# Two narrow full-precision products of a decoder step spread over four column groups of TensorE

## The reference

```python
# layer 0: 16 "rank" columns, widened to 512 by a second matrix
q, k, v, r, a_lr = jnp.split(x @ w_in, [QK_W, 2 * QK_W, 2 * QK_W + V_W, 2 * QK_W + 2 * V_W], axis=-1)
log_a = jax.nn.log_sigmoid((a_lr @ w_a2 + b_a).astype(F32)) / GLA_TAU
...
# layer 1: 16 gate columns, 8 for the input gate and 8 for the forget gate
q, k, v, o_pre, g_pre = jnp.split(x @ w_in, [QK_W, 2 * QK_W, 2 * QK_W + V_W, 2 * QK_W + 2 * V_W], axis=-1)
g = GATE_CAP * jnp.tanh((g_pre + b_gate).astype(F32) / GATE_CAP)
i_pre = g[..., :MLSTM_HEADS]
log_f = jax.nn.log_sigmoid(g[..., MLSTM_HEADS:])
```

## Time and profile before

| | |
|---|---|
| median of three runs | 1518.46 us |
| profiled execution | 1519.5 us, of which 1517.7 us are the span of its instructions |
| PE busy | 1500.7 us, 99% |
| DVE busy | 1216.1 us, 80% |
| ACT busy | 1010.2 us, 67% |
| DMA | 449.97 MB, 296 GB/s on average |
| granted TensorE clock | 0.997 of full on average |

### The profile page before, as it was taken

The page is one execution under the profiler, slowest core; times in us unless marked ns, Lnnn a source line. Parts: engine busy times, 40 slices in busy tenths (PEclk is TensorE's granted clock), DMA queues, the critical chain, the costliest instruction groups (busy, mean ns, idle before and its releaser), DMA issues.

```text
span 1517.7 us, 22956 instructions
## 1 busy us (share of the span) xinstructions
PE 1500.7 (99%) x8499; PEld 1189.8 (78%) x8499; DVE 1216.1 (80%) x1182; ACT 1010.2 (67%) x872; POOL 189.8 (13%) x229
## 2 busy tenths in 40 slices
PE   9999999999999999999999999999999999999997
PEld 7999999999998977777777776776776776777775
DVE  6858766646767588888888888888888888888888
ACT  5646533325556487787787777777778778778776
POOL 3334200002235140000000000000000000000010
PEclk9999999999999999999999999999999999999999
DMA  7467555455444689999999999999999999999993
GB/s 217 141 202 235 165 168 169 162 171 183 140 136 132 244 305 379 378 354 392 376 343 394 376 358 382 376 367 376 379 374 362 379 380 360 377 381 354 390 372 130
DMA packets 234263, 449.97 MB, mean 296 GB/s; under 512 B 16712, under 2 KB 83344, under 8 KB 234208
## 3 DMA queue, kind: packets, MB, share of 16 engines
q1 hardware_dynamic: 226208, 422.98, 77.9%
q0 software_dynamic: 7376, 24.53, 5.6%
q10 hardware_dynamic: 624, 1.70, 0.3%
HBM read 434.62 MB, written 14.57 MB: 296 GB/s over the span
## 4 chain that ended last, share of the span: by engine, by line
PE 93%; DVE 4%; ACT 1%; issue 1%; DMA 0%; SPq 0%; DVEq 0%; ACTq 0%
PE bank L1105 29%; PE bank L1107 28%; PE bank L1106 28%; PE bank L1762 1%; PE bank L1353 1%; DVE ring_lo L2314 1%; PE bank L1342 0%; PE bank L1696 0%; PE bank L1676 0%; PE bank L1791 0%; DMA par_rows<-in_mlstm_g_norm_dram 0%; DVE work L2273 0%; PE bank L1333 0%; PE bank L1254 0%; PE bank L1661 0%
## 5 line engine op out<-in xcount | busy, mean ns | idle before, releaser
L2906 DVE TENSOR_TENSOR w_lo<-ring,w_hi 128x2048 fp32r<-128x2048 f32 x337 | 771.4, 2291 | 121.4 <-ACT w_hi L2181 119.9
L2181 ACT ACTIVATE w_hi<-ring 128x2048 fp32r<-128x2048 f32 x337 | 645.4, 1918 | 223.3 <-PE bank L1107 223.2
L1105 PE MATMUL bank<-w_hi,xg_hi 128*96 128x512 f32 x896 | 355.6, 397 | 1.0 <-DVE xg_lo L2916 1.0
L1107 PE MATMUL bank<-w_hi,xg_lo 128*96 128x512 f32 x896 | 353.8, 395 | 0.0
L1106 PE MATMUL bank<-w_lo,xg_hi 128*96 128x512 f32 x896 | 351.6, 392 | 0.0
L1107 PE MATMUL bank<-work_split,ring_lo 128*128 128x288 f32 x920 | 270.7, 294 | 0.0
L1105 PE MATMUL bank<-work_split 128*128 128x288 f32 x904 | 268.6, 297 | 0.9 <-DVE ring_lo L2358 0.4
L1106 PE MATMUL bank<-work_split 128*128 128x288 f32 x904 | 265.9, 294 | 0.0
L1107 PEld LDWEIGHTS bank<-w_hi,xg_lo 128*96 128x96 f32 x896 | 144.4, 161 | 62.9
L1105 PEld LDWEIGHTS bank<-w_hi,xg_hi 128*96 128x96 f32 x896 | 144.5, 161 | 61.3 <-DVE w_lo L2906 2.0
L1106 PEld LDWEIGHTS bank<-w_lo,xg_hi 128*96 128x96 f32 x896 | 145.0, 162 | 59.9
(11 more groups left out here) (463 smaller groups left out, 1670.9 us busy)
## 6 DMA issues: line engine op xcount, KB each, us to landing
ring<-in_moe_w_gu_dram SPq DMA_DIRECT2D x225, 1024.0 KB, 6.6
ring<-in_moe_w_down_dram SPq DMA_DIRECT2D x112, 1024.0 KB, 6.4
ring<-in_ffn_w_gu_dram SPq DMA_DIRECT2D x22, 1024.0 KB, 5.1
ring<-in_gla_w_in_dram SPq DMA_DIRECT2D x12, 1024.0 KB, 5.5
ring<-in_mlstm_w_in_dram SPq DMA_DIRECT2D x12, 1024.0 KB, 5.3
ring<-in_ffn_w_down_dram SPq DMA_DIRECT2D x8, 1024.0 KB, 5.1
out_dram<-work POOLq DMA_DIRECT2D x9, 512.0 KB, 4.6
work<-in_state_gla_S_dram POOLq DMA_DIRECT2D x8, 512.0 KB, 7.2
```

Source lines behind the costliest of these rows:

```text
L1105: pe.matmul(out, w_hi_, x_hi, start=first, stop=False, skip_group_check=True)
L1107: return pe.matmul(out, w_lo_, x_hi, start=False, stop=last, skip_group_check=True)
L2181: ac.activation(w_hi[:, j % SPLIT, :], src, ACT.Copy).then_inc(whi_ready, 1)
L2906: ve.tensor_tensor(w_lo[:, j % SPLIT, :], src, w_hi[:, j % SPLIT, :].bitcast(F32), ALU.subtract)\
```

## The change

Both narrow products become `group_rows`. Block kt is multiplied by a weight of 32 columns, and its result goes to column group kt mod 4, PSUM partitions 32 (kt mod 4) to 32 (kt mod 4) + 31. So each product leaves four partial sums. Columns 16 to 31 of the weight are zero.

In layer 0 the four partial sums are summed by the next product: ACT copies all 128 rows, `w_a2` is loaded eight times, one below the other, and L0z is 128 rows deep. In layer 1 ACT copies the 128 rows, and one product with a wider `fold` sums them and puts the forget gates at partition 32; it is placed inside key tile k0, behind its block 3 (12 of 24 matmuls). DVE then reads this product's bank.

The weights of the two products share one buffer. The gate weights come in one small load instead of four, behind load 10 and after a wait for the rank rows. Seven more copies of `w_a2` are small loads of SP ahead of load 3. POOL fills zero columns once more at the start and makes the wider `fold` with four more steps.

```diff
         else:
             pj("g")
+            use("L1gf", 4)
             pj("k0")
...
-        fold = sb("fold", [P, MH])
+        fold = sb("fold", [P, GATE_ROW + MH])
...
-        w_lr = sb("w_lr", [P, KT, RANK])
-        w_gate = sb("w_gate", [P, KT // 4, 2, 4, MH])
-        w_a2 = sb("w_a2", [RANK, QK])
+        w_lr = sb("w_lr", [P, KT, GROUP])
+        w_gate = w_lr
+        w_a2 = sb("w_a2", [P, QK])
...
-        lr_sb = rank_rows[0:RANK, 9, :]
-        den_sb = rank_rows[:, 9, :]
+        lr_sb = rank_rows[:, 9, :]
+        den_sb = lr_sb
...
-                    small(w_lr[:, :, :], ins["gla_w_in"][0, :, 3072:3088].rearrange("(t p) n -> p t n", p=P))
-                    small(w_a2[:, :], ins["gla_w_a2"][0])
+                    small(w_lr[:, :, 0:RANK], ins["gla_w_in"][0, :, 3072:3088].rearrange("(t p) n -> p t n", p=P))
+                    for r in range(P // RANK):
+                        small(w_a2[r * RANK:(r + 1) * RANK, :], ins["gla_w_a2"][0])
...
-                if 4 <= i < 8:
-                    a, g = divmod(i - 4, 2)
-                    small(w_gate[:, a, g, :, :], ins["mlstm_w_in"][0, a * 4 * P:(a + 1) * 4 * P, 3072 + g * MH:3072 + (g + 1) * MH]
-                          .rearrange("(t p) n -> p t n", p=P), late_loaded)
+                if i == 10:
+                    sp.wait_ge(*full("L0lr"))
+                    small(w_gate[:, :, 0:2 * MH], ins["mlstm_w_in"][0, :, 3072:3072 + 2 * MH].rearrange("(t p) n -> p t n", p=P), late_loaded)
...
+            c(gp.memset(w_lr[:, :, RANK:GROUP], 0.0))
...
+            def group_rows(bk, w, l):
+
+                for kt in range(KT):
+                    pe.wait_ge(h_ready, KT * l + kt + 1)
+                    r = kt % 4 * GROUP
+                    mm = pe.matmul(bk[r:r + GROUP, 0:T], w[:, kt, :], hT[:, kt, :], start=(kt < 4), stop=(kt >= 4), skip_group_check=True)
                 return mm
...
-            end(rows_of(bk, w_lr, hT, 0, KT, RANK), "L0lr")
+            end(group_rows(bk, w_lr, 0), "L0lr")
...
-            for kt in range(KT):
-                pe.wait_ge(h_ready, KT + kt + 1)
-                mm = pe.matmul(bk[0:GATE_ROW + MH, 0:T], w_gate[:, kt // 4, :, :, :].rearrange("p g c n -> p (g c n)")
-                               [:, kt % 4 * MH:kt % 4 * MH + GATE_ROW + MH], hT[:, kt, :], start=(kt == 0), stop=(kt == KT - 1))
-            normed[0] = None
-            end(mm, "L1g")
-            for m in range(4):
+            end(group_rows(bk, w_gate, 1), "L1g")
+
+            def fold_gates():
+
+                pe.wait_ge(*copied("L1g"))
+                pe.wait_ge(fold_ready, N_FOLD)
+                bk = begin("L1gf")
+                end(pe.matmul(bk[0:GATE_ROW + MH, 0:T], fold[:, :], lr_sb[:, :], start=True, stop=True), "L1gf")
+
+            qk_tile("L1", "k", 0, {3: fold_gates})
+            for m in range(1, 4):
                 qk_tile("L1", "k", m)
...
-            free(ac.activation(lr_sb[:, :], take("L0lr")[0:RANK, 0:T], ACT.Copy), "L0lr")
+            free(ac.activation(lr_sb[:, :], take("L0lr")[:, 0:T], ACT.Copy), "L0lr")
...
-            ac.wait_ge(*copied("L1g"))
+            free(ac.activation(lr_sb[:, :], take("L1g")[:, 0:T], ACT.Copy), "L1g")
+            ac.wait_ge(*copied("L1gf"))
...
-            bk = take("L1g")
+            bk = take("L1gf")
```

More of the change, by code:

```diff
@@ L555, in trunk_kernel @@
         out_stored = sem("out_stored")
-        N_CONST = 42
+        N_CONST = 43
         N_FIRST = 5
-        N_FOLD = 5
-        N_SMALL = 16 * 8
-        N_LATE = 16 * 12
+        N_FOLD = 9
+        N_SMALL = 16 * (7 + P // RANK)
+        N_LATE = 16 * 9
         S_DONE = 16 * S_FIRST
@@ L905, in make_fold @@
                 gp.memset(fold[:, :], 0.0).then_inc(fold_ready, 1)
-                for r in range(4):
-                    gp.wait_ge(fold_ready, r + 1)
-                    gp.affine_select(out=fold[:, :], in_=fold[:, :], compare_op=ALU.not_equal, fill=1.0, base=-GROUP * r,
-                                     pattern=[[-1, MH]], channel_multiplier=1).then_inc(fold_ready, 1)
+                n = 1
+                for g in range(2):
+                    out = fold[:, GATE_ROW * g:GATE_ROW * g + MH]
+                    for r in range(4):
+                        gp.wait_ge(fold_ready, n)
+                        gp.affine_select(out=out, in_=out, compare_op=ALU.not_equal, fill=1.0, base=-(GROUP * r + MH * g),
+                                         pattern=[[-1, MH]], channel_multiplier=1).then_inc(fold_ready, 1)
+                        n += 1
+                assert n == N_FOLD
             def add_squares(i):
@@ L1074, in _ @@
                 end(mm, f"x{kt}")
-            normed = [None]
             def norm_of_sum(i, name):
@@ L1082, in norm_of_sum @@
                 end(pe.matmul(bk[:, 0:T], ones[:, :], hT[:, 0, :], start=True, stop=True), name)
-                normed[0] = i // 2
             def norm(i, name):
@@ L1091, in norm @@
                 end(mm, name)
-                normed[0] = i // 2
-            def rows_of(bk, w, src, c, n, m):
-                for kt in range(n):
-                    if normed[0] is not None:
-                        pe.wait_ge(h_ready, KT * normed[0] + kt + 1)
-                    mm = pe.matmul(bk[0:m, 0:T], w[:, kt, c:c + m], src[:, kt, :], start=(kt == 0), stop=(kt == n - 1))
-                normed[0] = None
+            def group_rows(bk, w, l):
[3 more added lines that the diff above has]
+                    mm = pe.matmul(bk[r:r + GROUP, 0:T], w[:, kt, :], hT[:, kt, :], start=(kt < 4), stop=(kt >= 4), skip_group_check=True)
                 return mm
@@ L1139, in first_tile, with qk_tile @@
                 end(sq, "L0ss")
-                normed[0] = 0
             qk_weights = [None]
-            def qk_tile(l, which, m):
+            def qk_tile(l, which, m, inside={}):
                 g = 2 * int(l[1])
@@ L1155, in qk_tile @@
                                kt == 0, kt == KT - 1)
+                    if kt in inside:
+                        inside[kt]()
                 end(mm, f"{l}{which}{m}")
@@ L2603, in _ @@
             mixer_lo(2, 3)
-            bk = take("L1g")
+            bk = take("L1gf")
             ve.tensor_scalar(rows[:, 0, :], bk[0:MH, 0:T], b_i[:, 0:1], None, ALU.add)
-            free(ve.tensor_scalar(rows[:, 1, :], bk[GATE_ROW:GATE_ROW + MH, 0:T], b_f[GATE_ROW:GATE_ROW + MH, 0:1], None, ALU.add), "L1g")
+            free(ve.tensor_scalar(rows[:, 1, :], bk[GATE_ROW:GATE_ROW + MH, 0:T], b_f[GATE_ROW:GATE_ROW + MH, 0:1], None, ALU.add), "L1gf")
             ve.wait_ge(tanh_ready, 2)
```

## The result

The changed kernel takes 1522.88 us (median of 18 runs, 1520.02 to 1526.22). 18 runs of the kernel before, beside it, have a median of 1520.28 us (1518.34 to 1522.91). The ratio is 1.0019, 95% interval 1.0012 to 1.0026: slower by 2.6 us, against the forecast of 0.9 us faster. The time lies above the stated range of 1515.7 to 1519.7, and above the 1521.5 from which on the prediction had 5%. The profiled execution took 1524.22 us, its span is 1522.4 us, and its mean granted clock is 0.993 against 0.997.

A forecast was written before the change was run, and what follows sets the result against it. The prediction took DVE's releases to bound the kernel. The median 1518.46 us less 0.87 from layer 0, or the profiled 1519.5 less 2.09 with the clock, gave 1517.5 us, with layer 1 adding nothing; range 1515.7 to 1519.7.

The forecast's parts named there:

- What bounds the kernel: Whole kernel: DVE's releases set the pace although PE is busy 1500.7 of 1517.7 us, so saved PE time becomes waiting.
- The grouped product: Rank rows and gate rows: 16 records in four column groups take 1.01 us, saving PE 2.98 and 3.00 us.
- the rival without overlap: Both narrow products: column groups do not overlap, layer 0 gives nothing, and the result is 1518.7 us; 5% chance.
- drains at a switch of tiling mode: Both grouped products: each pays two drains, which lie in pauses PE has anyway, so the sum stays.
- Layer 0: Before k0: PE waits about 2 us for DVE's weight slot, k0 starts 0.87 us earlier, and L0z costs the same.
- No fall at k1: Layer 0, k1: the 128-row L0z may remove the clock's fall; 1.56 us for PE, both effects 2.09 us at most.
- So the 0.87 us should arrive at layer 1.: From layer 0 to layer 1: PE and DVE both move by 0.87 us and the lead lasts.
- Layer 1, the release: Before layer 1's k0: DVE's weight slot at 380.24 releases it, so k0 starts 1.22 us earlier after a 1.7 us pause.
- it costs nothing, with 1.8 us of cover: Layer 1, inside k0: folded rows are ready at about 382.7 us, before DVE asks at 384.50.
- the new pauses lower the clock: Rival: the pause before layer 0's k0 brings the lower clock, k0 takes 1.56 us longer, result 1519.2 us; 16% chance.
- the base: Starting time of the sum: the kernel before at 1518.46 us, the median of three runs, taken as without the clock's fall.
- SP: Load queue at the start: seven more small issues at 0.43 us each, 3.0 us in all, stay hidden.

The follow-up runs named there:

- same_layout_fill: The full change with the work area kept at its old address, plus five products of constants in layer 1's pause; 1517.77 us, ratio 0.9988 to the kernel before.
- fill_layer1: The full change plus five products of constants between layer 1's gate rows and k0; 1521.44 us, ratio 1.0008 to the kernel before.
- fold_wide: The kernel before with only the fold buffer widened to 40 columns, moving later buffers by 128 bytes; 1522.14 us, ratio 1.0014.
- same_layout: The full change with the wide fold matrix placed elsewhere, so the work area keeps its old address; 1520.37 us, ratio 0.9996 to the kernel before.
- two_blocks: The kernel before with layer 1's gate product over two of its eight blocks, without groups, copy or fold product; 1520.45 us, ratio 1.0002.
- layer0_only: The kernel before with only layer 0's part of the change, layer 1 and the fold matrix as before; 1518.91 us, ratio 0.9987.
- layer1_only: The full change with layer 0's rank rows summed in one group and w_a2 loaded once; 1524.50 us, ratio 1.0029 to the kernel before.
- deep_rank: The kernel before with only L0z made 128 rows deep and w_a2 loaded eight times; 1520.14 us, ratio 0.9996.
- layer0_192: The kernel before with layer 0's part of the change and the work area 192 bytes along; 1519.63 us, ratio 0.9995.

## Why the prediction was wrong

*What bounds the kernel.* Right. Nearly all that TensorE saves turns into waits for DVE, in both layers, and neither the full 6 us nor a part of 3 us reached the end in any kernel.

*The grouped product.* Right: 16 records within 1.18 us in both layers. From its first record to the start of a product that follows without a pause it takes 1.11 us (same_layout_fill, 378.76 to 379.87), against 1.01 forecast and 3.99 before. That excludes the rival without overlap. The rule of the Trainium skill, "TensorEngine Tiling (Array Packing)", section "Key Properties", on drains at a switch of tiling mode was put as harmless to the sum. The trace agrees that a switch costs time, and little: behind the grouped product the first full-width record of fill_layer1 starts 0.34 us after the last grouped one and its own successor 0.35 us later, where such records otherwise are 0.24 apart. That is 0.2 us for the way back. The kernel before paid as much between its rank rows and k0 (0.34 and 0.24 us, where 0.24 and 0.13 are usual), so the sum stays.

*Layer 0.* Right in mechanism, with one term missed. The pause was 1.78 us and ended by line 2321, the counterpart of 2314. k0 came 1.02 us nearer (forecast 0.87). L0z was put at the same cost within 0.1 us, and that is the term: the reading that depth isn't dearer holds for the single record, but going to the 16-row form and back cost 0.39 us. No fall at k1, as hoped. The lead came to 2.3 us against 2.09. (By the prediction's own working the clock alone would be worth 1.22 us to vt4, 63.59 less 62.37, and not 1.25.)

*"So the 0.87 us should arrive at layer 1."* **This step failed**, by way of a term that the sum didn't have. The lead shrank by 2.0 us between 136 and 379 us, because the widened fold matrix moved the split weights by 128 bytes and each of the some 75 tiles there grew by 0.027 us. fold_wide shows this alone at 1.0014, and same_layout shows the change without it at 0.9996, where the forecast had 0.9994. The prediction costed what each edit executes and nothing for where its buffers lie.

*Layer 1, the release.* **Wrong in its releaser.** The prediction had k0 wait for the weight slot at 380.24. It is held by DVE's second read-out of q2, whose bank k0 takes, and which in the kernel before ended at 381.19. It lies in the stretch that the earlier trace rows leave out, between 378.04 and 384.50:

```profile
380.73 0.46 DVE L2591 TENSOR_TENSOR work<-bank,rbc 64x288 f32<-64x288 f32 x1
```

So k0 could come only some 0.3 us nearer in place of 1.22, and the pause was 2.50 us in place of 1.7. two_blocks shows the same wait with nothing of the change in it (k0 at 381.33).

*Layer 1, "it costs nothing, with 1.8 us of cover".* **Wrong.** The folded rows came at 386.6 and DVE stood 0.71 us for them. The late k0 took 0.9 us of the cover and the low clock the rest and more: k0 with the fold took 5.42 us. Kept busy instead (fill_layer1), it took 4.06 us and nothing was lost.

*The clock.* The rival "the new pauses lower the clock" had 16% and its rule from the Trainium skill, "TensorE: Matmul & The Clock Gate", section "Why this matters for your kernels". The trace agrees with it where TensorE was busy for 0.90 of 3.40 us and the clock then fell, and in layer0_only, layer1_only and two_blocks. The page's row is on longer gaps than these of 1.8 to 2.6 us, so here the measurement goes further than the rule. It isn't certain for each pause: six of seven at layer 0 and one of four at layer 1 had no fall. The prediction priced it in layer 0 and hid most of it in layer 1; it was in layer 1 that it cost. It also took the median runs to be without any fall. Of 32 runs of the kernel before in one set only one had a mean clock of 0.998 (1518.6 us); the median was 1520.31. Over all sets 12 of 93 runs had it, and they took 1518.56 to 1519.03 us. That alone puts the base 1.8 us too low, and the range with it: two of the three runs behind the base, 1518.34 and 1518.46, were as fast as these, which was bad luck.

*SP.* Right: eight issues of w_a2 in 6.07 us, the last small issue at 18.69, and ACT's wait for load 3 shorter than before.

```profile
10.29 6.07 SPq L705 DMA_DIRECT2D w_a<-in_gla_w_a_dram  x8
...
18.69 0.29 SPq L705 DMA_DIRECT2D m_chunk<-in_state_mlstm_m_dram  x1
```
```profile
26.61 1.92 ACT L1891 ACTIVATE work_split<-ring 128x2048 fp32r<-128x2048 f32 x1 [1.59 <-DMA ring<-in_gla_w_in_dram]
```

*The sum, from the experiments.* Layer 0's part -0.13%, the place of the buffers +0.14%, layer 1's part +0.15% (layer1_only less fold_wide). That makes +0.16%, against +0.19% measured; each term is uncertain by about 0.1%. At the old addresses layer 1's part comes out smaller, +0.09% (same_layout less layer0_only).

*The sum, from the runs at full clock.* Runs with a mean clock of 0.998 leave most falls out, and tell the parts apart more sharply than the medians do. Against 1518.56 to 1519.03 us of the kernel before, fold_wide took 1520.64 to 1521.25, layer0_only 1517.39 to 1517.70, the one such run of same_layout 1517.42, and the one of the kernel after 1520.02. So at full clock, as far as single runs can say it, the change is about 1.3 us faster at the old addresses (forecast: 0.87) and about 1.3 us slower with the buffers moved.

What stays open, first: the late start. The rank rows came 1.8 to 3.7 us later than in the kernel before in five of the eight profiled executions with the 128-row w_a2 and in one of the twelve others. In four of these six the granted clock was low somewhere between 9.3 and 19.6 us; in the other two the trace has no clock record before 18.3 us. The added loads can't have begun it in all of them: in deep_rank the clock was low from 9.32 us, and in same_layout_fill and layer0_192 the first eight transposes took 0.41 us each in place of 0.29, before SP issued the first of these loads at 10.3 to 10.7 us. But five of eight against one of twelve may be more than chance, and no experiment was made for it.

Second: the fall of the clock between 461 and 465 us, worth 1.5 to 1.6 us. It is in seven of the twelve kernels whose work area lies elsewhere modulo 256 bytes than in the kernel before, and in one of the eight where it lies as there. Whether TensorE's lag brings it wasn't tested, so a part of what the medians charge to the place may be this fall.

## What to carry to other kernels

When an edit changes the size of a buffer, compare the pace of products that it doesn't touch before looking for a cause in those it does; keep the addresses of the operands of the busiest products fixed, or pad. Where another engine's release follows closely behind a product, shortening that product makes a pause, so look up *every* release of the next tile (its bank as well as its weights), and count on a fall of the clock behind the pause unless something keeps TensorE busy (layer 1: three of four unfilled pauses, none of three filled). When the gain is under 0.1%, three runs of the kernel before are no base.

## What the hardware showed

- A split tile of 24 matmuls with 288 columns takes 3.147 to 3.200 us in layer 0 and 3.120 to 3.200 us in the FFN, by where the work area lies modulo 256 bytes. Between two of these places it was the place of the high weight parts that counted. The expert loop changed by up to 1.1 us in 976, with its best places not those of the tiles.
- The records of a full-precision product start 0.242 us apart at 16 rows and at 128, but going to the 16-row form from 128-row matmuls and back costs 0.39 us.
- Sixteen full-precision records of 32 columns in four column groups take 1.11 us, and 16 or 40 columns wide in one group 3.99 to 4.01. Within a round of four they start 0.007 us apart, and the rounds 0.24 to 0.27.
- Tile k1 behind the 16-row L0z ran at the lower clock in six of twelve executions, behind the 128-row one in none of eight.
- Five products of constants, 2.69 us of no use, went with a layer 1 tile of 4.04 to 4.06 us in three of three executions; without them it took 4.04 us once and 5.42 and 5.58 us where the clock fell. With the old addresses they gave the lowest median here, 1517.77 us.
